# Tokens loaded and turned in four quarters by column halves, first sums of squares behind the high parts, VectorE rounding the first half slab

## The reference, cut to what matters

```
xn   = x * rsqrt(mean(x*x) + eps) * attn_norm_g      # x: 256 x 1024
proj = xn @ w_in                                     # sliced in gq, gk, mq, mk, mv, gv, gr, and a gate of rank 16
log_a = log_sigmoid(gate @ w_gate_up + b_gate) / 16  # gate = the last 16 columns of proj
```

## Time and profile before

| | us |
|---|---|
| median of 3 runs | 720.66 |
| profiled execution, device time | 720.59 |
| its span, first to last instruction | 718.9 |
| TensorE busy | 713.1 |
| TensorE weight loads busy | 630.3 |
| VectorE busy | 558.0 |
| ScalarE busy | 376.5 |
| GpSimd busy | 54.2 |

### The profile page before, as it was taken

The page is one execution under the profiler, slowest core; times in us unless marked ns, Lnnn a source line. Parts: engine busy times, 40 slices in busy tenths (PEclk is TensorE's granted clock), DMA queues, the critical chain, the costliest instruction groups (busy, mean ns, idle before and its releaser), DMA issues.

```text
span 718.9 us, 11332 instructions
## 1 busy us (share of the span) xinstructions
PE 713.1 (99%) x4394; PEld 630.3 (88%) x4394; DVE 558.0 (78%) x669; ACT 376.5 (52%) x463; POOL 54.2 (8%) x61
## 2 busy tenths in 40 slices
PE   9999999999999999999999999999999999999998
PEld 8998887888888888989999888998988888888886
DVE  5979777989998889987578877987788666566573
ACT  7645476675555455565556454544465433443341
POOL 1346000001220000021000000000000000000000
PEclk9999999999999999999999999999999999999999
DMA  8865424356555555446335444454527545554521
GB/s 350 307 194 183 134 101 176 119 180 229 185 217 182 177 190 210 142 145 248 119 126 178 170 171 176 148 200 180 214 79 250 215 179 182 191 210 176 180 114 58
DMA packets 19609, 129.18 MB, mean 180 GB/s; under 512 B 2288, under 2 KB 2544, under 8 KB 4976
## 3 DMA queue, kind: packets, MB, share of 16 engines
q1 hardware_dynamic: 19424, 128.51, 49.6%
q10 hardware_dynamic: 144, 0.10, 0.1%
HBM read 126.50 MB, written 1.05 MB: 177 GB/s over the span
## 4 chain that ended last, share of the span: by engine, by line
PE 98%; DMA 1%; ACT 0%; issue 0%; DVE 0%; SPq 0%
PE ps L1868 21%; PE ps L1844 14%; PE ps L1845 14%; PE ps L1846 14%; PE ps L1876 11%; PE ps L1888 8%; PE ps L1890 4%; PE ps L2081 1%; DMA h<-in_x 1%; PE ps L2104 1%; PE ps L2111 1%; PE ps L1816 1%; PE ps L1801 1%; PE ps L1910 1%; PE ps L1926 1%; PE ps L1917 1%
## 5 line engine op out<-in xcount | busy, mean ns | idle before, releaser
L651 ACT ACTIVATE hiw<-raw 128x2048 fp32r<-128x2048 f32 x116 | 222.0, 1915 | 200.8 <-PE ps L1876 97.8
L1106 DVE TENSOR_TENSOR low<-raw,hiw 128x2048 fp32r<-128x2048 f32 x116 | 267.4, 2309 | 65.1 <-ACT hiw L651 64.5
L1868 PE MATMUL ps<-xx,hiw 128*128 128x512 f32 x656 | 156.1, 390 | 0.0
L1868 PEld LDWEIGHTS ps<-xx,hiw 128*128 128x128 f32 x656 | 121.6, 188 | 24.2
L1876 PEld LDWEIGHTS ps<-xx,low 128*128 128x128 f32 x656 | 83.9, 191 | 3.0
L1876 PE MATMUL ps<-xx,low 128*128 128x256 f32 x656 | 85.2, 283 | 0.0
L1844 PE MATMUL ps<-hiw,yhi 128*128 128x512 f32 x208 | 81.9, 394 | 0.0
L1845 PE MATMUL ps<-low,yhi 128*128 128x512 f32 x208 | 81.2, 390 | 0.0
L1846 PE MATMUL ps<-hiw,ylo 128*128 128x512 f32 x208 | 81.0, 389 | 0.0
L1430 DVE TENSOR_REDUCE arena<-ps 128x512 f32<-128x1024 f32 x41 | 50.1, 1221 | 24.1 <-PE ps L1876 24.0
L1844 PE MATMUL ps<-xx,hiw 128*128 128x256 f32 x240 | 68.8, 286 | 0.0
(11 more groups left out here) (283 smaller groups left out, 971.0 us busy)
## 6 DMA issues: line engine op xcount, KB each, us to landing
raw<-in_slabs SPq DMA_DIRECT2D x116, 1024.0 KB, 4.8
vec<-in_vec SPq DMA_DIRECT2D x1, 1258.5 KB, 7.5
cst<-in_cst SPq DMA_DIRECT2D x1, 1220.0 KB, 13.2
h<-in_x SPq DMA_DIRECT2D x2, 512.0 KB, 4.3
raw<-in_slabs SPq DMA_DIRECT2D x2, 512.0 KB, 6.6
arena<-arena SPq DMA_DIRECT2D x16, 64.0 KB, 4.7
out<-h SPq DMA_DIRECT2D x1, 512.0 KB, 2.7
out<-h SPq DMA_DIRECT2D x2, 256.0 KB, 2.0
```

The costliest lines, as they stand in the source:

```text
L651: act.activation(hiw[:, n % SPLIT, :], raw[:, n % RAW, :], ACT.Copy).then_inc(hi_made, 1)
L1106: dve.tensor_tensor(low[:, n % SPLIT, :], raw[:, n % RAW, :], hiw[:, n % SPLIT, :].bitcast(F32), ALU.subtract).then_inc(lo_made, 1)
L1868: pe.matmul(banks[:, c, :], hi[:, kt, cc_], xx[:, kt].rearrange("p a b -> p (a b)"), start=kt == 0, stop=False)
```

## The change

The token load is cut in four: columns 0 to 511 of both token tiles first, then columns 512 to 1023 of both. TensorE turns them in that order, four blocks per quarter, so that the first two banks are full after two quarters. The zeros are multiplied 5 times, not 7. ScalarE starts with the eight `xhi`, then does `first_sum(0)`, the second half slab's high part and `first_sum(1)`; VectorE makes the high part of the first half slab, between its fourth and fifth `xlo`. TensorE's last eight matmuls of the gate product are cut in two: four stay in their place, four go behind the first 16 matmuls of slab 0. GpSimd scales level 1 right behind its differences, and not in the pass of level 2.

```
-WARM = 7
+WARM = 5
-            sp.dma_start(h[:, 0, :], x_in[0:P, :]).then_inc(s("x0_in"), 16)
-            sp.dma_start(h[:, 1, :], x_in[P:T, :]).then_inc(s("x1_in"), 16)
+            for half in range(2):
+                for tt in range(TT):
+                    cols = slice(half * D // 2, (half + 1) * D // 2)
+                    sp.dma_start(h[:, tt, cols], x_in[tt * P:(tt + 1) * P, cols]).then_inc(s(f"x{tt}_in{half}"), 16)
...
-                if i >= 2:
+                if i == 1:
+                    scale_level(i)
+                elif i > 2:
                     scale_level(i - 1)
...
-                act.wait_ge(s(f"x{tt}_in"), 16)
+                for half in range(2):
+                    act.wait_ge(s(f"x{tt}_in{half}"), 16)
...
-            first_sum(0)
             act.wait_ge(s("vec_gains_in"), 16)
             first_turned()
-            act.wait_ge(s("half_in"), 16)
-            act.activation(row_half(hiw[:, 0, :], 0), row_half(raw[:, 0, :], 0), ACT.Copy).then_inc(s("half_hi"), 1)
+            first_sum(0)
             act.wait_ge(raw_full[0], 16)
...
-            first_turned()
+            first_turned(range(KT // 2))
+            dve.wait_ge(s("half_in"), 16)
+            dve.tensor_copy(row_half(hiw[:, 0, :], 0), row_half(raw[:, 0, :], 0)).then_inc(s("half_hi"), 1)
+            first_turned(range(KT // 2, KT))
...
-                for tt in range(TT):
-                    pe.wait_ge(s(f"x{tt}_in"), 16)
-                    for kt in range(KT):
-                        o = bank(f"n0_{kt // 2}")[:, kt % 2 * T + tt * P:kt % 2 * T + (tt + 1) * P]
-                        mm = pe.transpose(o, h[:, tt, kt * P:(kt + 1) * P], ident)
+                for half in range(2):
+                    for tt in range(TT):
+                        pe.wait_ge(s(f"x{tt}_in{half}"), 16)
+                        for kt in range(half * KT // 2, (half + 1) * KT // 2):
+                            o = bank(f"n0_{kt // 2}")[:, kt % 2 * T + tt * P:kt % 2 * T + (tt + 1) * P]
+                            mm = pe.transpose(o, h[:, tt, kt * P:(kt + 1) * P], ident)
...
                 for half, high_made in enumerate(((s("half_hi"), 1), (hi_made, 1))):
+                    if half:
+                        first_product_low(range(KT // 2, KT))
                     pe.wait_ge(*high_made)
...
-                for kt in range(KT):
+                first_product_low(range(KT // 2))
+
+            def first_product_low(kts):
+
+                for kt in kts:
                     turned(0, kt)
-                    mm = pe.matmul(o, smh[:, kt, cols], xlo[:, kt, :], start=False, stop=kt == KT - 1)
-                mm.then_inc(*fills("gg"))
+                    mm = pe.matmul(bank("gg")[:, 0:T], smh[:, kt, 0:128], xlo[:, kt, :], start=False, stop=kt == KT - 1)
+                    if kt == KT - 1:
+                        mm.then_inc(*fills("gg"))
```

More of the change, by code:

```diff
@@ L1124, in first_level_scaled, with first_turned @@
                 dve.tensor_tensor(late, late, level_halves(gqT, 0)[1], ALU.mult).then_inc(s("first_scaled"), 1)
-            def first_turned():
-                for kt in range(KT):
+            def first_turned(kts):
+                for kt in kts:
                     dve.wait_ge(s("xhi_made"), (kt | 1) + 1)
@@ L1784, in first_turn @@
                 pe.wait_ge(s("ident_made"), 1)
-                for tt in range(TT):
-                    pe.wait_ge(s(f"x{tt}_in"), 16)
-                    for kt in range(KT):
-                        o = bank(f"n0_{kt // 2}")[:, kt % 2 * T + tt * P:kt % 2 * T + (tt + 1) * P]
-                        mm = pe.transpose(o, h[:, tt, kt * P:(kt + 1) * P], ident)
-                        if tt == TT - 1 and kt % 2:
-                            mm.then_inc(*fills(f"n0_{kt // 2}"))
+                for half in range(2):
[4 more added lines that the diff above has]
+                            mm = pe.transpose(o, h[:, tt, kt * P:(kt + 1) * P], ident)
+                            if tt == TT - 1 and kt % 2:
+                                mm.then_inc(*fills(f"n0_{kt // 2}"))
             def turn_tile(n, tt):
```

## The result

The changed kernel takes 722.60 us in the median of 11 runs (721.21 to 723.29), the kernel before beside it 720.74 (11 runs, 720.55 to 721.35). The ratio is 1.0022, with a 95% interval of 1.0014 to 1.003 (the medians alone give 1.0026): slower by 1.9 us, where the forecast was 1.3 us faster and the range ended at 720.3. The spread of the changed kernel is itself a finding: 2.1 us from its lowest to its highest, against 0.8.

What follows compares the result with a forecast made beforehand. TensorE's path was taken as the bound, with the entrance chain (second token tile, turn, ScalarE's moves, gate product) ahead. -1.25 - 0.11 = -1.36, less 0.05 for near-even pairs: -1.3 us, 719.35; range 718.8 to 720.3.

Steps and rivals of the forecast that it cites:

- Loads: Token loads at the entrance: second quarter lands at 4.7 us (4.6 to 4.8), fourth at 6.1 (5.95 to 6.25).
- the term of the sum, -1.25: Entrance: ScalarE starts at 5.27 instead of 6.52 us, so the gate product's first part ends 1.25 us earlier.
- The rival on late quarters: Token loads: half slab at 8.75 or second quarter at 5.1 us, gain only 0.7 to 1.1, 719.6 to 720.0; chance 0.12.
- Turn and xhi: Token turns and ScalarE's eight moves: start 0.57 us after the second quarter, ScalarE's pace decides, -1.25 us.
- Low part of the gate product: Gate product's last eight matmuls: the first four run in 0.48 us without the stall, -0.11 us.
- First half slab on VectorE: VectorE's rounding copy: half slab lands at 7.9 to 8.75 us, copy takes 0.75, 0.4 spare, nothing on the path.
- ScalarE's order: ScalarE's sums after the moves: spread factors ready at 13.4 us, wanted at 13.65, cover only 0.3, no wait.
- Fewer zeros: TensorE's start: two fewer zeros cost nothing if the clock rises where it did.
- late clock, slower: TensorE's turns and gate product: level stays low, with a rise at 11.3 us +0.9 us, 721.5; chance 0.04.
- GpSimd's order: GpSimd's scaling of level 1, moved to near 27 to 30 us: zero, bounds 0 and +0.5 us.

Runs made afterwards that it cites:

- e11: The changed kernel with 9 zeros instead of 5: 721.01 us, ratio 1.0001.
- e1: The changed kernel with 7 zeros instead of 5, all else kept: 721.08 us, ratio 1.0002.
- e13: The changed kernel with 9 zeros and the first slab's load held until the second token quarter is in: 721.07 us, ratio 1.0002.
- e3: The changed kernel with whole token tiles and 7 zeros: 720.57 us, ratio 0.9994.
- e5: The kernel before (7 zeros, its own order) with the change's four token quarter loads: 723.13 us, ratio 1.0029.
- e6: The kernel before with the tokens in four transfers of 64 whole 4 KB rows each: 723.21 us, ratio 1.0029.
- e12: The kernel of e5 with the first slab's load issued only when all four quarters are in: 722.63 us, run once.
- e10: The changed kernel with two column-half token transfers, 9 zeros, and turns block column by block column: 720.21 us, ratio 0.9991.
- e14: The kernel of e10 with the first slab's load held until the first column half is in: 720.45 us, ratio 0.9992.

## Why the prediction was wrong

The profiles can be taken apart from the last landing to the anchor: before 15.00 - 5.95 = 9.05 us; e11, high level, 15.65 - 8.24 = 7.41; after, low level, 16.99 - 8.14 = 8.85. So

- the last landing: 8.14 - 5.95 = +2.2
- the rest of the change, counted from the last landing: 7.41 - 9.05 = -1.6
- the lower level: 8.85 - 7.41 = +1.4

in all +2.0, the span's 2.0. The three add up by construction; what carries them are the runs that change one thing each. For the middle term e1 is a second witness, 15.38 - 8.0 = 7.38. That -1.6 is no gain that an early landing would keep: it is large because the last quarter is so late that all work on the first two is long done. In e13, with the last quarter at 6.8, the same stretch is 8.8, as the wait for VectorE's copy has come into it. By whole runs the same in three steps: orders alone (e3) -0.3 in the medians and about -0.2 in the lowest executions, quarters on top (e1 against e3) +0.5, two zeros fewer (result against e1) +1.5; in all +1.7, the result's 1.9 being from other executions.

Step by step:

- *Loads*: the step that failed first. "The fourth at 6.1 (5.95 to 6.25)" was 8.14, the second 5.05 where the bounds ended at 4.8. I bounded the rows and not the number of transfers, and argued that the bytes in the queue, not the issues, set the landings. e5 and e6 show in its place that four transfers land 2 us late, and e12 that 1.3 of it come from loads issued behind them and moved ahead of the last quarter's end; the rest is a slower queue. With the landings goes the term of the sum, -1.25. The rival on late quarters named this place, with 5.1 for the second, but priced it at 0.2 to 0.6 us and left the fourth alone, which was 2.2 late. Even the best landings tried here, in e10, started ScalarE only 0.44 us earlier than before (6.08 against 6.52), for 0.5 us in the median. By the rule of the Trainium skill on small descriptors (DMA: Bandwidth & Descriptors, Why small descriptors are slow) the rows alone would hardly move a landing. No run here sets the rows apart from the rest, so the runs don't decide on it.
- *Turn and xhi*: ScalarE's pace held, 0.36 us each; it started 0.57 behind the landing in the forecast and 1.11 after (6.16 - 5.05), mostly as the turns ran at the lower level: in e11, with the turns at the higher, it was 0.7. With the fourth quarter so late it was no longer the bound.
- *Low part of the gate product*: right, 0.47 for each four, no stall.
- *First half slab on VectorE*: the copy took 0.69 (0.75 forecast), in both e13 and after. It landed at 9.67 (2.67 + 7.0), outside my 7.9 to 8.75 and past the 8.5 where the cover ends. It cost nothing only because the quarters were later still. In e13, with the quarters earlier and its own load held back, this wait is the one that ends last.
- *ScalarE's order*: right. The spread factors were there at 15.2, wanted at 16.99.
- *Fewer zeros*: the step that failed second. The cover, "if the clock rises where it did", was gone: 1.4 to 1.5 us. The rival "late clock, slower" had the mechanism and, by luck as the moment differs from execution to execution, the moment too (11.3 us forecast, 11.43 to 11.63 in the profile). It had a chance of 0.04, and its +0.9 was worked out for the early landings. Its row was in hand, all 14 zeros at the lower level and the turn at the higher. I took it that 2.5 us of zeros would do as 3.4 did, and had no row for it. The Trainium skill (TensorE: Matmul & The Clock Gate, Part 1) holds that the moment is the chip's own; e3's long execution agrees, with a rise at 10.66.
- *GpSimd's order*: zero, as forecast. The two residuals beside it take 5.02 us together where they took 4.48, and TensorE's list has no new wait.
- The rivals were treated as exclusive. Here both came at once, and together they lie outside a range made of either.

What stays open: why later loads are moved ahead of the last quarter, and why the queue is slower with four transfers; whether the zeros or the idle stretch behind them matter for the level; and what in a given execution sets the moment of the rise. The runs show that last one only as a spread.

## What to carry to other kernels

Cutting a load into more transfers did not bring the last part as early as the whole: price the landing of each part with what is issued behind it. Work that seems to hide in idle time may be what lifts TensorE's level; before taking it away, look in the spacing of like matmuls where the rise lies. And where a kernel's own executions spread by 1 to 2 us, take ten of them, and read which of them the profile shows.

## What the runs showed of the hardware that was not expected

- The granted clock read 1.00 in all stretches where matmuls of 256 columns were 0.21 us apart instead of 0.12.
- With the same 7 zeros and whole tiles TensorE was at the higher level at 4.75 us in one profiled execution (before) and rose at 10.66 in another, of a near kernel (e3), whose times spread by 1.6 us (720.40 to 722.03).
- A 256 KB transfer in the queue's fourth place took 5.7 us to land with loads issued behind it (e5) and 4.4 without (e12). From 5.0 to 6.0 us, 197 GB/s were moved in the changed kernel with four token transfers, and 385, then 328, in the kernel before with two.
- A 512 KB half slab held back until about 5.1 us took 5.05 us to land behind quarters (e13) and 4.1 behind halves (e14).
